# First normalisation of a two-block model kernel: its root applied behind the first projection, with first loads and splits cut into single outputs

## The reference, cut to what matters

```python
def rms_norm(x, g):
    xf = x.astype(jnp.float32)
    y = xf * lax.rsqrt(jnp.mean(xf * xf, axis=-1, keepdims=True) + RMS_EPS)
    return (y * g.astype(jnp.float32)).astype(x.dtype)
...
    u = h @ w_pw1 + b_pw1                       # h = rms_norm(x, mix_pre_g[0]); 1024 -> 2048
    a, gate = jnp.split(u, 2, axis=-1)
    u = a * jax.nn.sigmoid(gate)
    u = jnp.pad(u, ((0, 0), (CONV_WIDTH - 1, 0), (0, 0)))
    u = lax.conv_general_dilated(u, w_dw[:, None, :], ...) + b_dw     # 31 taps over the tokens
    u = jax.nn.silu(layer_norm(u, ln_g, ln_b))
    return u @ w_pw2 + b_pw2
```

## Time and profile before

| what | us |
|---|---|
| median of 3 runs | 1212.76 |
| lowest, highest | 1208.52, 1216.09 |
| the profiled execution | 1209.91 |
| its span in the profile | 1208.1 |

### The profile page before, as it was taken

The page is one execution under the profiler, slowest core; times in us unless marked ns, Lnnn a source line. Parts: engine busy times, 40 slices in busy tenths (PEclk is TensorE's granted clock), DMA queues, the critical chain, the costliest instruction groups (busy, mean ns, idle before and its releaser), DMA issues.

```text
span 1208.1 us, 26351 instructions
## 1 busy us (share of the span) xinstructions
PE 1160.0 (96%) x10538; PEld 993.7 (82%) x10538; DVE 848.7 (70%) x1390; ACT 669.8 (55%) x1024; POOL 213.5 (18%) x166
## 2 busy tenths in 40 slices
PE   8999999999899999999999999999999999999997
PEld 6888888888666888888877678888887777888886
DVE  5656876655864886555677468888777665888775
ACT  5435566433656566433565566665556656666542
POOL 0000000000002000000032433554231333355400
PEclk8999999999999999999999999999999999999999
DMA  7871355555251355555232334554465334455452
GB/s 292 275 243 65 118 222 208 209 207 195 86 209 71 139 209 210 209 189 190 108 106 106 139 140 156 217 215 152 175 242 196 109 116 179 162 209 211 142 196 78
DMA packets 22250, 208.37 MB, mean 172 GB/s; under 512 B 2464, under 2 KB 8992, under 8 KB 9120
## 3 DMA queue, kind: packets, MB, share of 16 engines
q1 hardware_dynamic: 22176, 207.32, 47.4%
HBM read 205.09 MB, written 2.23 MB: 172 GB/s over the span
## 4 chain that ended last, share of the span: by engine, by line
PE 54%; issue 17%; DVE 12%; POOL 6%; ACT 6%; DMA 4%; SPq 0%; POOLq 0%; DVEq 0%; ACTq 0%
PE ps L654 13%; PE ps L656 13%; PE ps L655 13%; POOL tmp L1941 5%; DVE w_lo L2013 4%; DMA staged<-weights 3%; ACT w_hi L1384 2%; POOL probs L1950 1%; PE ps L812 1%; PE ps L665 1%; PE ps L667 1%; PE ps L835 1%; PE ps L666 1%; PE ps L710 1%; PE ps L787 1%
## 5 line engine op out<-in xcount | busy, mean ns | idle before, releaser
L1384 ACT ACTIVATE w_hi<-staged 128x2048 f16<-128x2048 f32 (+1 forms) x192 | 356.2, 1870 | 196.9 <-PE ps L656 156.1
L2013 DVE SCALAR_TENSOR_TENSOR w_lo<-staged,w_hi 128x2048 f16<-128x2048 f32 (+1 forms) x192 | 429.3, 2249 | 44.1 <-ACT w_hi L1384 43.9
L654 PE MATMUL ps<-f_hi,w_hi 128*128 128x256 f16 x1596 | 435.1, 273 | 4.4 <-DVE w_lo L2013 2.1
L656 PE MATMUL ps<-f_hi,w_lo 128*128 128x256 f16 x1596 | 435.0, 273 | 0.0
L655 PE MATMUL ps<-f_lo,w_hi 128*128 128x256 f16 x1596 | 435.0, 273 | 0.0
L654 PE MATMUL ps<-x_hi,w_hi 128*128 128x256 f16 x928 | 253.8, 274 | 5.8 <-DVE x_lo L2043 2.9
L655 PE MATMUL ps<-x_lo,w_hi 128*128 128x256 f16 x928 | 253.4, 273 | 0.0
L656 PE MATMUL ps<-x_hi,w_lo 128*128 128x256 f16 x928 | 253.4, 273 | 0.0
L654 PEld LDWEIGHTS ps<-f_hi,w_hi 128*128 128x128 f16 x1596 | 156.1, 98 | 25.1 <-issue 3.4
L655 PEld LDWEIGHTS ps<-f_lo,w_hi 128*128 128x128 f16 x1596 | 156.2, 98 | 18.3
L656 PEld LDWEIGHTS ps<-f_hi,w_lo 128*128 128x128 f16 x1596 | 156.2, 98 | 18.1
(11 more groups left out here) (304 smaller groups left out, 1588.9 us busy)
## 6 DMA issues: line engine op xcount, KB each, us to landing
staged<-weights SPq DMA_DIRECT2D x82, 2048.0 KB, 8.1
staged<-weights SPq DMA_DIRECT2D x16, 1408.0 KB, 6.2
qT<-u_rows SPq DMA_DIRECT2D x16, 143.0 KB, 3.2
kT<-u_rows SPq DMA_DIRECT2D x16, 143.0 KB, 3.7
staged<-weights SPq DMA_DIRECT2D x2, 1024.0 KB, 8.3
u_rows<-probs SPq DMA_DIRECT2D x8, 144.0 KB, 4.6
cst<-constants SPq DMA_DIRECT2D x1, 1031.5 KB, 16.2
h<-x_turned SPq DMA_DIRECT2D x1, 1024.0 KB, 5.2
```

Of the source, the lines that this page charges most:

```text
L654: pe.matmul(out, wh, xh[:, c, :], start=(c == 0), stop=False)
L656: last = pe.matmul(out, wl, xh[:, c, :], start=False, stop=(c == kc - 1))
L1384: act.activation(w_hi[:, s, o:o + n], staged[:, s, o:o + n], ACT.Copy, scale=SW).then_inc(hi_split, 1)
L2013: dve.scalar_tensor_tensor(w_lo[:, s, o:o + n], staged[:, s, o:o + n], SW, w_hi[:, s, o:o + n], ALU.mult, ALU.subtract).then_inc(lo_split, 1)
```

## The change

The gain of the first norm joins the gains that are scaled by 4 at the start, and x_hi and x_lo are made of x times gain, without the root. The squares are added by GpSimd; their sum, the root and its spreading are put inside output 3 of the projection, and the scale is copied to `LATE_SCALE`. For each chunk DVE multiplies gate and value sums by it (`late_pair`) from PSUM into `tmp`, and the sigmoid and m read `tmp`.

Unit 0 is loaded and split in four single outputs of 1024 columns (512 KB), unit 1 in halves, x in two parts of 512 KB. The order of the loads is new, and three of SyncE's issues wait for earlier landings. The second part of the constants and the positions are loaded behind unit 7. The first three chunks have PSUM banks of their own, then two pairs of banks take turns. All eight chunks now go through `glu_chunk`, `keep_warm` runs nine times before the first and no more behind the sums. ACT loads its tables by two operations on one column (root, then sigmoid). The diff, cut to its core (blank lines left out):

```diff
-SCALED_GAINS = ("ffn_pre_0", "mix_pre_1", "kv_in", "ffn_pre_1", "attn_0", "ffn2_0", "attn_1", "ffn2_1")
-VECTORS = [*((_name, DC) for _name in SCALED_GAINS), ("mix_pre_0", DC), ("mix_post_0", DC), ("mix_post_1", DC),
+SCALED_GAINS = ("mix_pre_0", "ffn_pre_0", "mix_pre_1", "kv_in", "ffn_pre_1", "attn_0", "ffn2_0", "attn_1", "ffn2_1")
+VECTORS = [*((_name, DC) for _name in SCALED_GAINS), ("mix_post_0", DC), ("mix_post_1", DC),
...
-LATE = ("ffn_pre_0", "mix_pre_1", "ffn_pre_1", "attn_0", "ffn2_0", "attn_1", "ffn2_1")
-LATE_ADDED = ("ffn2_0", "attn_1", "ffn2_1")
+LATE = ("mix_pre_0", "ffn_pre_0", "mix_pre_1", "ffn_pre_1", "attn_0", "ffn2_0", "attn_1", "ffn2_1")
+LATE_ADDED = ("mix_pre_0", "ffn2_0", "attn_1", "ffn2_1")
...
+        def glu_bank(j):
+            return 2 * j if j < 3 else 2 * ((j - 3) % 2)
+        def glu_freed(j):
+            return {3: 1, 4: 2}.get(j, j - 1) if j >= 3 else 0
...
-            sp.dma_start(h[:], x_dram).then_inc(x_loaded, 16)
-            early = CCOL["mla_mask"]
-            sp.dma_start(cst[:, 0:early], const_dram[:, 0:early]).then_inc(cst_loaded, 16)
-            gains = VCOL["taps"]
-            sp.dma_start(vec[:, 0:gains], vec_dram[:, 0:gains]).then_inc(vec_loaded, 16)
-            def load(u, s):
-                sp.dma_start(staged[:, s:s + 1, :], w_stream[bass.ds(u, 1)].rearrange("u p n -> p u n")).then_inc(
-                    landed[s], 16)
-            for e in range(2):
-                half = slice(HALF * e, HALF * e + HALF)
-                sp.dma_start(staged[:, 0, half], w_stream[0, :, half]).then_inc((landed_early, landed[0])[e], 16)
-            load(1, 1)
-            sp.dma_start(vec[:, gains:], vec_dram[:, gains:]).then_inc(taps_loaded, 16)
-            sp.dma_start(cst[:, early:], const_dram[:, early:]).then_inc(late_loaded, 16)
-            sp.dma_start(posi[:], pos_dram).then_inc(late_loaded, 16)
+            gains, early = VCOL["taps"], CCOL["mla_mask"]
+            def first_output(q):
+                at = slice(D * q, D * q + D)
+                sp.dma_start(staged[:, 0, at], w_stream[0, :, at]).then_inc(landed_early[q % 2] if q < 3 else landed[0], 16)
+            sp.dma_start(vec[:, 0:gains], vec_dram[:, 0:gains]).then_inc(early_loaded, 16)
+            first_output(0)
+            for q in range(2):
+                sp.dma_start(h[:, 4 * q:4 * q + 4, :], x_dram[:, 4 * q:4 * q + 4, :]).then_inc(x_loaded[q], 16)
+            first_output(1)
+            sp.wait_ge(early_loaded, 16)
+            sp.dma_start(cst[:, 0:early], const_dram[:, 0:early]).then_inc(early_loaded, 16)
+            sp.wait_ge(landed_early[0], 16)
+            first_output(2)
+            first_output(3)
+            sp.wait_ge(landed_early[1], 16)
+            sp.dma_start(staged[:, 1, 0:HALF], w_stream[1, :, 0:HALF]).then_inc(landed_early[1], 16)
+            sp.dma_start(staged[:, 1, HALF:], w_stream[1, :, HALF:]).then_inc(landed[1], 16)
+            sp.wait_ge(early_loaded, 32)
+            sp.dma_start(vec[:, gains:], vec_dram[:, gains:]).then_inc(early_loaded, 16)
...
             early_unit(7)
+            sp.dma_start(cst[:, early:], const_dram[:, early:]).then_inc(late_loaded, 16)
+            sp.dma_start(posi[:], pos_dram).then_inc(late_loaded, 16)
...
-            pe.wait_ge(dve_step, 2)
-            keep_warm(7)
-            pe.wait_ge(cst_loaded, 16)
-            sums("mix_pre_0")
-            spread_scale("mix_pre_0", inverted, NORM_AT["mix_pre_0"] + 1)
-            keep_warm(4)
-            together("pw1", 2, x_hi, x_lo, normed("mix_pre_0"))
+            pe.wait_ge(dve_step, 1)
+            keep_warm(9, 7)
             def glu_chunk(j):
                 u, s = FIRST["pw1"] + j // 2, (FIRST["pw1"] + j // 2) % 2
+                def norm_sums(c):
+                    if c == 1:
+                        pe.wait_ge(early_loaded, 32)
+                        sums("mix_pre_0")
+                    if c == 6:
+                        spread_scale("mix_pre_0", inverted, NORM_AT["mix_pre_0"] + 1)
                 for e in range(2):
                     n = 2 * j + e
-                    if e == 0:
+                    if j < 2 and e == 0:
+                        pe.wait_ge(early_lo, j + 1)
+                    elif e == 0 or j < 2:
                         arrived(2 * u + j % 2)
-                    if j >= 2:
-                        pe.wait_ge((drained["pw1"], glu)[e], j - 1)
-                    features(ps[:, n % RING, 0:T], s, n % 4 * DC * P, DC, x_hi, x_lo).then_inc(product["pw1"], 1)
+                    if j >= 3:
+                        pe.wait_ge(drained["pw1"], 2 * glu_freed(j) - 1 + e)
+                    features(ps[:, glu_bank(j) + e, 0:T], s, n % 4 * DC * P, DC, x_hi, x_lo,
+                             normed("mix_pre_0") if n == 0 else norm_sums if n == 3 else None).then_inc(product["pw1"], 1)
...
+                if c == 0:
+                    pe.wait_ge(drained["pw1"], 6)
...
-            for j in range(1, DC):
+            for j in range(DC):
...
-            act.wait_ge(x_loaded, 16)
-            squares("mix_pre_0", h, lambda c: None)
+            def first_output(q):
+                act.wait_ge(landed_early[q % 2] if q < 3 else landed[0], 32 if q == 2 else 16)
+                at = slice(D * q, D * q + D)
+                act.activation(w_hi[:, 0, at], staged[:, 0, at], ACT.Copy, scale=SW).then_inc((early_hi, hi_split)[q % 2], 1)
+            def first_squares(chunks):
+                for c in chunks:
+                    act.activation(sq[:, c, :], h[:, c, :], ACT.Square).then_inc(squared, 1)
+            act.wait_ge(dve_step, 1)
+            act.activation(unused[:], decay_k[:, 0:1], ACT.Sqrt)
+            first_output(0)
+            act.wait_ge(tables_made, 1)
+            for c in range(DC):
+                act.wait_ge(x_loaded[c // 4], 16)
+                act.activation(x_hi[:, c, :], h[:, c, :], ACT.Copy, scale=v("mix_pre_0", c)).then_inc(x_hi_ready, 1)
+            first_output(1)
+            first_squares(range(4))
+            first_output(2)
+            first_output(3)
+            first_squares(range(4, DC))
+            split(2)
             root("mix_pre_0")
-            split(0)
-            his("mix_pre_0", x_hi, 0, 3)
-            split(1)
-            his("mix_pre_0", x_hi, 3, DC)
-            for g in range(2, 4):
-                split(g)
+            act.activation(unused[:], k("rms_eps"), ACT.Sigmoid)
+            split(3)
...
             u0 = FIRST["pw1"]
-            act.wait_ge(tables_made, 1)
+            act.wait_ge(tables_made, 2)
             for j in range(DC):
-                act.wait_ge(product["pw1"], 2 * j + 1)
+                act.wait_ge(drained["pw1"], 2 * j + 1)
                 if j >= 2:
                     act.wait_ge(glu, j - 1)
-                act.activation(m[:, 2 * (j % 2), :], ps[:, 2 * j % RING, 0:T], ACT.Sigmoid, bias=v("b_pw1", DC + j),
-                               scale=INV).then_inc(drained["pw1"], 1)
+                act.activation(m[:, 2 * (j % 2), :], tmp[:, j % 2, :], ACT.Sigmoid, bias=v("b_pw1", DC + j)).then_inc(
+                    gate_ready, 1)
                 act.wait_ge(glu, j + 1)
                 if j >= U_RING:
                     act.wait_ge(u_shifted[j - U_RING], SHIFTED)
                 act.activation(glu_parts[:, j % U_RING, 0, TAPS - 1:TAPS - 1 + T], m[:, 2 * (j % 2) + 1, :], ACT.Copy,
-                               scale=INV * SX).then_inc(u_hi_ready, 1)
+                               scale=SX).then_inc(u_hi_ready, 1)
...
-            pool.wait_ge(late_loaded, 32)
+            add_squares("mix_pre_0")
...
+            step(dve.memset(decay_k[:], 0.0))
             dve.memset(pad[:], 0.0)
             dve.memset(logf_rows[:], 0.0)
-            chain(dve.memset(decay_k[:], 0.0))
-            step(dve.memset(probs[:], 0.0))
+            dve.wait_ge(early_loaded, 16)
+            at = slice(VCOL[SCALED_GAINS[0]], VCOL[SCALED_GAINS[-1]] + DC)
+            dve.tensor_scalar(vec[:, at], vec[:, at], SX, None, ALU.mult).then_inc(tables_made, 1)
+            dve.memset(probs[:], 0.0)
+            def first_output(q):
+                dve.wait_ge((early_hi, hi_split)[q % 2], q // 2 + 1)
+                at = slice(D * q, D * q + D)
+                dve.scalar_tensor_tensor(w_lo[:, 0, at], staged[:, 0, at], SW, w_hi[:, 0, at], ALU.mult,
+                                         ALU.subtract).then_inc((early_lo, lo_split)[q % 2], 1)
+            first_output(0)
+            dve.wait_ge(tables_made, 1)
+            for c in range(DC):
+                low("mix_pre_0", c, (x_hi, x_lo))
+            first_output(1)
+            first_output(2)
+            first_output(3)
+            at = slice(VCOL["b_dw"], VCOL["b_dw"] + DC)
+            dve.tensor_scalar(vec[:, at], vec[:, at], 1.0 / INV, None, ALU.mult).then_inc(tables_made, 1)
+            split(2)
+            split(3)
             invert("mix_pre_0")
-            dve.wait_ge(vec_loaded, 16)
```

(21 more changed lines are left out.)

40 lines of the change are left out of this document (18 added, 22 removed).

## The result

The changed kernel takes 1221.14 us (median of 6 runs, 1217.5 to 1223.24), the kernel before in the same comparison 1211.32 (6 runs): 1.0088 times as long, 95% interval 1.0065 to 1.0111. It is slower, by 9.8 us. The forecast was 3.5 us slower. The direction was right and the time lies in the stated range (1207 to 1222), near its upper end. It lies outside the narrower range that the prediction gave for its own sum (1212 to 1219). The size was not right, and the rest of this text is mostly about the missing 6 to 7 us.

The account below looks back on a forecast made before the run. It took a closed loop of DVE and ACT, not TensorE, to bound the stage before the layer norm. Loop +4.6, start -1.1 and tail 0 gave +3.5 us on the median of 1212.8, written as 1216; range 1207 to 1222.

Parts of the forecast that it names:

- The loop: DVE and ACT per chunk: pair and sigmoid before m lengthen a step from 6.18 to 7.12 us, +4.6 over seven.
- Rival A: Chunk loop: pair and sigmoid fit DVE's idle time, steps stay 6.18, the early start carries, 1209.8 us; chance 0.16.
- The last add: Start, GpSimd's sum of squares: the last of seven adds ends at 19.5 us, between 16.7 and 20.7.
- walk by turns: Start: GpSimd's adds and DVE's w_lo take turns after each instruction, so the last two adds end at 20.7 us.
- Rival C: Start: no collisions on GpSimd, last add at 16.7, total +0.7 us, 1213.5; chance 0.12.
- one rate of 396 KB per us: Start, loads: every landing comes at 3.36 + KB/396 us, x at 6.2 and 7.5.
- From the last add to m(0): End of the start: sum, root, table load, unit 1's splits, reciprocal, spread and first pair take 10.1 us together.
- The tail: From the last chunk's m to the layer norm: stays as it is, 16.3 us.
- rival B: Last two conv blocks: TensorE pauses some 4 us, clock drops, 1.7 us more, +5.2 in all, 1218; chance 0.16.
- Moved transfers: Constants' second part and positions, loaded at about 100 us behind unit 7: cost 0, or +2.9 us without cover.
- Rival D: MLP weights: the moved transfers hold up unit 8, +2.9 us more, 1219; chance 0.06.
- the same three terms: Stage up to the layer norm: start to m(0) -1.1, seven loop steps +4.6, unchanged tail 0; sum +3.5 us.

Follow-up runs that it names:

- e1: Changed kernel with the next chunk's pair of multiplications moved on DVE to behind the low part, ahead of w_lo: 1215.38 us, 1.0047 times the kernel before.
- e3: Changed kernel with six of GpSimd's seven adds on one column, leaving squares out of the sum: 1217.07 us, 1.0045 times the kernel before.
- e5: Changed kernel with TensorE summing the squares again and GpSimd's adds dropped: 1216.59 us, 1.0055 times the kernel before.
- e7: Changed kernel with x issued first, and x_hi and x_lo ahead of the work on output 0: 1221.24 us, 1.0092 times the kernel before.
- e2: Changed kernel with DVE's reciprocal and copy of the scale ahead of the last w_lo of unit 1: 1221.19 us, 1.0092 times the kernel before.
- e4: Changed kernel with nine filler matmuls in TensorE's pause ahead of conv block 5: 1218.42 us, 1.0061 times the kernel before.
- e6: Changed kernel with the edits of e1 and e5, small work reordered and the scale spread earlier: 1206.42 us, 0.9957 times the kernel before.
- e8: Changed kernel with the edits of e1 and e2 together: 1213.2 us, 1.0021 times the kernel before.

## Why the prediction was right in direction and short in size

The stated range held, but that says little for the sum. It reached up to 1222 only because the rivals and the 4 us by which single runs differ had been put on top; the sum's own bounds ended at 1219, and 1221.14 is above them. That the time would stay within 1% held, just (1.0088, with an interval up to 1.0111).

**The loop: right, by seven times 0.13 short.** The mechanism is shown by e1: put the pair in DVE's idle time and the step is 6.18 again. The step measured 7.25, not 7.12. The sigmoid that reads SBUF takes 0.51 us (mean 508 ns), and the prediction used the 0.46 of the one that reads PSUM. The rest, the larger part, is hand-overs: from the pair's start to m are 1.08 us (39.79 to 40.87), of which 0.42 and 0.51 are work and 0.15 hand-overs, where the prediction had 0.06. Rival A is out for this kernel, though e1 shows that it needs only the other place in the order.

**The last add: 23.1, not 19.5, and this is the largest error.** Two steps failed. First, the prediction's own walk by turns gave 20.7, and it then took 19.5 "nearer to the end with collisions". There was no reason for taking less than the walk. With ACT 2.5 us late (next point) the walk gives 23.2; 23.1 was measured. The chain of waits shows the turns, add by add; in one of them the walk had the order the other way round, the fifth add ahead of half 2's w_lo and not behind it, which changes nothing in the sum (changed kernel, start, length, what):

```profile
14.33 0.73 POOL stat L1976
...
15.20 1.54 POOL stat L1976
...
16.87 1.54 POOL stat L1976
...
18.54 2.85 POOL stat L1976
...
21.53 0.73 POOL stat L1976
...
22.39 0.73 POOL stat L1976
```

Beside DVE's 1024-column w_lo an add takes 1.54 us, beside the 2048-column one 2.85, alone 0.73. By the rule that the prediction cites (the Trainium skill, SBUF — State Buffer, "Who interferes with whom") each of the two blocks the other for a whole instruction, and the trace agrees in both directions: DVE's two w_lo took 3.27 us instead of the 2.36 of e3 and e5. The operation on 8 columns behind them took 0.70 us instead of 0.17, and ended with the add beside it (18.43 and 18.41), though it reads only one tile. What DVE loses was in the walk's turns, but not in the prediction's times for DVE (w_lo of output 3 done at 14.5; measured 17.8). Rival C (no collisions) is out.

Second, ACT reached the squares late. x_hi began at 8.09 and not 6.2 (it varied from 7.13 to 8.09 over nine executions with this order of issue), and took 3.30 us for eight and not 2.6. The prediction had every landing by one rate of 396 KB per us; in the first us the rate is lower (139 to 336 GB/s from 2 to 6 us, 377 and more from 6.5 on), so x came 1.8 us late. With x issued first, in e7, it was 396 GB/s from 4 to 8 us, and 309 in the changed kernel; so the order of the pieces matters, but how is not shown. That the delay carries over to the last add one for one is seen across executions: from the start of x_hi to the end of the last add are 15.0, 14.8, 14.8 and 15.0 us in the changed kernel, e1, e2 and e4. And the prediction priced x_hi by the row of the squares (0.32 a step), but x_hi scales by a vector of gains. The kernel before has such rows, for a later norm (its groups by form):

```profile
L1620 ACT ACTIVATE x_hi<-h,vec 128x256 f16<-128x256 f32 x8 | 3.3, 492 | 0.0
```

**From the last add to m(0): right.** 10.5 us, forecast 10.1. Here the clock is in it too: behind the reciprocal DVE waited 1.31 us for the spread, and 0.80 in e3, with the clock at 0.50 and 0.71 from 24 to 28 us. e6 shows that most of this was a matter of order: there root to m(0) is 5.0 us, against 9.3.

**The tail: "stays as it is" failed.** It grew by 2.05 us. This is rival B (forecast for the two blocks: +1.7; three ran behind the pause), which came on top of the forecast and not in its place, and e4 shows it as the clock. The prediction had the pause of some 4 us in its text, and put the clock's loss into a rival where it belonged in the sum. It had also missed that conv block 5 waits for ACT's conv_out(2). That TensorE began its first product at 9.36 and not at 8.3 cost nothing.

**Moved transfers: right** (0). Rival D is out.

So the sum would have been 2.95+5.5+2.05 = +10.5 by the same three terms. The terms were the right ones. The errors all had one sign: for the sigmoid, x_hi and the landings the cheapest like row or rate was taken, for the adds less than the walk, and for the clock nothing.

What stays open: the 3.7 us that e6 loses behind the layer norm's start. About 1.3 are in the layer norm up to the spread, where the clock was 0.50 to 0.77 for 8 us and the one-column products took 5.07 us instead of 3.73; the rest is spread over later stages in pieces of about one us. e5 has a similar loss (1118.8 us behind the layer norm's start), and e1 and e8 have 1118.3. The clock in the layer norm doesn't explain it: e4's products took 5.31 us there, and e4 has the shortest remainder of all, 1115.0. Whether these losses follow from the kernel or are chance of single executions isn't settled.
